# Output bias times gates joins the residual rows ahead of the expert loop; a block's activations are turned inside the next up product; loads and lists moved

## The chip, the cores and the metric

The kernel runs on one core of a Trainium2 chip. The metric is the device time in microseconds (us) of one execution. The core's engines are TensorE (PE in the profile; PEld is its loading of weights into the array), VectorE (DVE), ScalarE (ACT), GpSimd (POOL) and SyncE (SP). SyncE computes nothing here: it issues most of the transfers (DMA), in program order, and waits ahead of some of them.

## The reference, cut to what matters

One layer: attention of two kinds, and then a mixture of experts on the attended rows. The part that the change touches is the second half.

```
h = h + mix @ w_out                          # 512 token rows of 1024, the residual rows
xf = rmsnorm(h, ffn_norm)
top_val, top_idx = top_k(xf @ w_router + b_router, 4)     # 4 of 32 experts
gates = softmax(top_val)
# for each token and each of its 4 experts e:
#   act = clamped_swiglu(xf @ w1[e] + b1[e])
#   y   = act @ w2[e] + b2[e]
#   h  += gate * y
out = rmsnorm(h, final_norm)                 # in float32
```

The sum over a token's experts of gate times b2[e] depends on the gates alone. It is a product of the 512 x 32 table of gates (zero where an expert isn't chosen) with the 32 x 1024 table b2.

## The kernel before, in words

Everything is written out by hand, engine by engine, with semaphores. SBUF holds one arena that is used again and again.

**Ahead of the loop.** TensorE makes the attended rows in eight parts (`out_part`, line 1540). VectorE adds them to the residual rows `res` (line 1040). For each of four tiles of 128 tokens ScalarE and VectorE work out the root, ScalarE scales the row, GpSimd multiplies by the gain (line 559), and SyncE stores the tile in a table `xfd` in HBM (line 467). The residual rows themselves go to another table in HBM, `acc` (line 464), to which the expert loop adds. `choose(t)` finds the four experts of each token of tile t (lines 1052 to 1067) and `weigh(t)` its gates, in three bfloat16 parts (lines 1069 to 1080), both on VectorE. Then experts are ordered, tokens are counted, and tables are made that say which expert each block of 32 tokens belongs to and where the experts' weights come in the sequence of loads (lines 1111 to 1199, with small products on TensorE, lines 1612 to 1630).

**The expert loop.** Each expert's tokens are cut into blocks of 32 slots; with this input there are 81 blocks. A block's rows are gathered from `xfd` by an indirect DMA that GpSimd issues (line 567). Per block g the loop on TensorE does this (`finish_block`, line 1690, then `up_of`, line 1668):

- turn the activations of block g, two 128x128 transposes (line 1694); ScalarE copies them out as `actT` (line 811),
- turn the gathered rows of block g + 2 (`turn_x`, line 1638); ScalarE copies them (line 793),
- `slot_product` (line 1619): the token list of a block further ahead,
- four products that put b2 of block g's expert into the output bank (line 1700), from `ball`, which holds b1 and b2 in bfloat16 parts,
- `down` (line 1684): the product with w2 on top of them,
- `up` of block g + 2 (line 1657) with w1, and its bias (line 1664).

So up(g + 1) and its bias stand right ahead of finish_block(g). The products with w1 and w2 put four matmuls of 32 output columns side by side in the array (128*32 in the rows); the transposes and the token list use it in full (128*128). VectorE clamps and gates the up product (`hidden`), makes token lists (`slot_rows`, `slot_list`) and scales the result by the gates (`outputs`, line 1224); GpSimd issues the indirect DMA that adds it to `acc` (line 575).

**Weights.** One expert's weights are 12.6 MB: four loads of 2.1 MB for w1 and two for w2. SBUF holds two experts (`par` 0 and 1). SyncE loads the experts in the order of their places. Line 490 (w1) waits until the last block of the expert two places back has read that quarter of the buffer (`w1_read`), line 495 (w2) until it has read that half. The first two experts are loaded ahead of the loop: six loads early, then lines 473, 479, 480 and 482 (six more). The six early ones are w1 of the first expert and half of w1 of the second. The residual rows `res` lie where the second quarter of the second expert's w1 goes (line 479), so that load waits until they are stored.

## Time and profile before

| | us |
|---|---|
| median of 3 runs | 1412.35 |
| lowest, highest | 1410.44, 1421.33 |
| the profiled execution | 1412.71 |
| its span, first to last instruction | 1410.9 |
| TensorE busy | 1304.0 (92%) |
| TensorE loading weights into the array | 636.4 (45%) |
| VectorE busy | 662.0 (47%) |
| chain that ended last: TensorE, DMA | 83%, 10% |
| moved by DMA | 459.18 MB |

A matmul's busy time is modelled and neighbours overlap, so 92% does not say that TensorE is at its peak. The expert loop runs from about 371 us to about 1386 us of the span. In the profile's 40 slices the sixteen DMA engines are busy to a tenth or less between 106 and 212 us, and to nine tenths or more in nearly all slices of the loop. A float32 matmul leaves two records in the trace, so `x64` on line 1657 is one block's up product of 32 matmuls; a transpose leaves one.

### The profile page before, as it was taken

Reading aid. Unit: us, or ns where it says so; the run is one execution under the profiler, and the core shown is the slowest. Engines: PE = TensorE matmul, PEld = TensorE weight load, DVE = VectorE, ACT = ScalarE, POOL = GpSimd, SP = SyncE. Lnnn points to the kernel's source line nnn. Section 1 sums busy time; section 2 is a strip of 40 time slices with the busy share of each in tenths; the row PEclk is TensorE's granted clock in tenths of the full one; section 3 lists DMA queues with packets and bytes.
Section 4 is the critical chain, followed back from the end, with each engine's and each line's share of the span. In section 5 each row is a group of like instructions: output and inputs, shape, how many; then the busy total and the mean of one; then the engine's idle time right before and its main releaser. Section 6 shows DMA issues by size and latency. Waiting matters only on the chain.

```text
span 1410.9 us, 36714 instructions
## 1 busy us (share of the span) xinstructions
PE 1304.0 (92%) x13322; PEld 636.4 (45%) x13323; DVE 662.0 (47%) x2250; ACT 292.9 (21%) x579; POOL 294.5 (21%) x464
## 2 busy tenths in 40 slices
PE   7999999989489996999999999997999899999992
PEld 4756665555134442444444444442444344444441
DVE  2114334655635552555555555552555355555555
ACT  2012223424111111111111111110111111111113
POOL 5310000002112221222222222221222122222221
PEclk9999999999699998999999999998999899999996
DMA  9520003426878999999999997999999999999994
GB/s 320 149 49 1 1 0 136 167 98 260 329 314 347 416 416 421 416 417 417 418 417 416 417 415 314 378 410 420 419 418 418 418 416 416 417 416 417 400 416 167
DMA packets 59952, 459.18 MB, mean 325 GB/s; under 512 B 8692, under 2 KB 9076, under 8 KB 27156
## 3 DMA queue, kind: packets, MB, share of 16 engines
q1 hardware_dynamic: 51364, 436.12, 74.8%
q0 software_dynamic: 8176, 22.36, 6.0%
q8 instruction: 19, 0.31, 0.1%
q10 hardware_dynamic: 384, 0.32, 0.1%
q14 instruction: 9, 0.07, 0.0%
HBM read 440.26 MB, written 18.51 MB: 325 GB/s over the span
## 4 chain that ended last, share of the span: by engine, by line
PE 83%; DMA 10%; DVE 3%; issue 2%; ACT 1%; POOL 0%; ACTq 0%; SPq 0%; POOLq 0%; DVEq 0%
PE PS L1657 38%; PE PS L1684 19%; DMA sb_arena<-in_w 7%; PE PS L1322 4%; PE PS L1316 4%; PE PS L1694 2%; PE PS L1319 2%; PE PS L1320 2%; PE PS L1516 2%; PE PS L1638 1%; PE PS L1664 1%; PE PS L1700 1%; PE PS L1367 1%; PE PS L1489 1%; DMA xfd<-sb_arena 1%
## 5 line engine op out<-in xcount | busy, mean ns | idle before, releaser
L1657 PE MATMUL PS<-sb_arena,sb_work 128*32 128x512 f32 x5184 | 590.4, 606 | 35.3 <-DMA sb_arena<-in_w 28.4
L1657 PEld LDWEIGHTS PS<-sb_arena,sb_work 128*32 128x32 f32 x5184 | 188.7, 112 | 386.5 <-issue 322.1
L1684 PE MATMUL PS<-sb_arena,sb_work 128*32 128x256 f32 x5184 | 296.8, 381 | 4.5
L1211 DVE TENSOR_SCALAR sb_work<-PS 128x256 f32<-128x256 f32 x81 | 34.3, 423 | 393.9 <-PE PS L1664 393.9
L1684 PEld LDWEIGHTS PS<-sb_arena,sb_work 128*32 128x32 f32 x5184 | 166.8, 110 | 110.8 <-issue 19.4
L811 ACT ACTIVATE sb_work<-PS 128x256 f32<-128x256 f32 x81 | 31.0, 383 | 814.3 <-PE PS L1694 814.3
L1224 DVE TENSOR_SCALAR sb_work<-PS,sb_gates 32x256 f32<-32x256 f32 x324 | 155.2, 479 | 14.7 <-PE PS L1684 1.2
L566 POOL TENSOR_TENSOR sb_sm<-sb_sm 128x1 f32<-128x1 f32 x85 | 16.7, 197 | 546.5 <-DVE sb_gidx L1166 546.5
L1136 DVE TENSOR_SCALAR sb_slots<-sb_ca,sb_b,sb_rk 128x128 bf16<-128x128 f32 x340 | 95.3, 367 | 59.1 <-issue 59.1
L575 POOL DMA_INDIRECT accd<-sb_work,sb_sidc x81 | 111.3, 1374 | 12.5 <-issue 1.1
L809 ACT ACT_TABLE_LOAD x81 | 103.9, 1283 | 1.4
L567 POOL DMA_INDIRECT sb_work<-xfd,sb_gidx x85 | 85.8, 1009 | 14.1 <-issue 3.8
L1316 PE MATMUL PS<-sb_arena 128*128 128x512 f32 x128 | 58.7, 600 | 1.7 <-DVE sb_arena L874 1.7
L574 POOL TENSOR_TENSOR sb_sm<-sb_sm 128x1 f32<-128x1 f32 x81 | 15.6, 193 | 213.1 <-DVE sb_sidc L1226 213.1
L1322 PE MATMUL PS<-sb_arena 128*128 128x512 f32 x128 | 58.6, 598 | 1.0 <-DVE sb_arena L896 1.0
L927 DVE TENSOR_TENSOR_SCAN sb_arena<-sb_arena 128x1344 f32<-128x1344 f32 x8 | 23.7, 2957 | 70.1 <-ACT sb_arena L665 70.1
L1694 PEld LDWEIGHTS PS<-sb_ca,sb_work 128*128 128x128 f32 x162 | 25.5, 207 | 53.4 <-issue 53.4
L1214 DVE TENSOR_TENSOR sb_work<-sb_work,PS 128x256 f32<-128x256 f32 x81 | 34.1, 421 | 29.3 <-ACT PS L798 29.2
L1694 PE MATMUL PS<-sb_ca,sb_work 128*128 128x128 f32 x162 | 40.9, 334 | 1.2 <-issue 1.1
L1319 PE MATMUL PS<-sb_arena 128*128 128x264 f32 x128 | 39.3, 389 | 0.0
L1320 PE MATMUL PS<-sb_arena 128*128 128x264 f32 x128 | 39.0, 386 | 0.0
L1638 PE MATMUL PS<-sb_ca,sb_work 128*128 128x128 f32 x166 | 34.0, 287 | 4.8 <-DMA sb_work<-xfd,sb_gidx 4.8
(253 smaller groups left out, 1170.5 us busy)
## 6 DMA issues: line engine op xcount, KB each, us to landing
sb_arena<-in_w SPq DMA_DIRECT2D x192, 2048.0 KB
sb_arena<-in_w_in SPq DMA_DIRECT2D x6, 2048.0 KB, 21.0
sb_arena<-in_x SPq DMA_DIRECT2D x8, 512.0 KB, 7.8
sb_arena<-in_w_out SPq DMA_DIRECT2D x2, 2048.0 KB, 12.1
accd<-sb_arena SPq DMA_DIRECT2D x4, 512.0 KB, 8.9
xfd<-sb_arena SPq DMA_DIRECT2D x4, 512.0 KB, 5.2
sb_arena<-accd SPq DMA_DIRECT2D x4, 512.0 KB, 5.4
out<-sb_arena SPq DMA_DIRECT2D x4, 512.0 KB, 3.5
```

Of the source, the lines that this page charges most:

```text
L567: pool.indirect_dma_start(out=xg[b], out_offset=None, in_=xfd, in_offset=bass.IndirectOffsetOnAxis(ap=gidx[:, b:b + 1], axis=0)).then_inc( ...
L575: pool.indirect_dma_start(out=acc, out_offset=bass.IndirectOffsetOnAxis(ap=sidc[0:SLOTS, b:b + 1], axis=0), in_=yb[b], in_offset=None, com ...
L809: act.preload_act_table(ACT.Sigmoid)
L1136: nc.vector.tensor_scalar(slots[:, t, :].rearrange("p (q s) -> p q s", s=SLOTS), ca[:, C_SLOT:C_SLOT + SLOTS].unsqueeze(1).to_broadcast([P ...
L1224: nc.vector.tensor_scalar(yb[b][:, c * QD:(c + 1) * QD], PS[rows, 4, 0:QD], gates[rows, bass.ds(n, 1)], None, ALU.mult).then_inc(y_ready, 1)
L1316: last = mm(PS[:, b, :], w[:, k, f * P:(f + 1) * P], nT[:, k, META:NKEY], **io)
L1319: mm(PS[:, b, 0:n], w[:, k, f * P:(f + 1) * P], nT[:, k, 0:n], **io)
L1320: last = mm(PS[:, b + 1, 0:n], w[:, k, f * P:(f + 1) * P], nT[:, k, n:NKEY], **io)
L1322: last = mm(PS[:, b, :], nT[:, k, META + f * P:META + (f + 1) * P], w[:, k, :], **io)
L1657: last = mm(PS[group(c), b, :].rearrange("p (a n) -> p a n", a=2), xT[:, k % 2, group(k // 2)], w[:, k, :, c, :], start=k == 0, stop=False)
L1684: last = mm(PS[group(n), 4, 0:QD], actT[:, k % 2, group(k // 2)], w[:, k, n * QD:(n + 1) * QD], start=False, stop=k == KT - 1)
L1694: last = nc.tensor.transpose(PS[:, 6, j * P:(j + 1) * P], pairs(gat[b], j), ident)
```

## The change

What it does, in the order of the program:

- **Gates as a float32 table.** `weigh` keeps the gates in `gw`. For tiles 2 and 3 the weighing moves from VectorE to GpSimd; ScalarE sums their four exponentials itself, and VectorE makes only the reciprocals.
- **Last tile of rows.** Scaling and gain of tile 3 become one instruction on VectorE, in place of one on ScalarE and one on GpSimd.
- **Bias into the residual rows.** TensorE turns the gates (`turn_gates`), multiplies each tile of `res` by the identity into two PSUM banks (`rows_part`, two matmuls) and adds gates times b2 (`bias_part`, two matmuls); ScalarE copies the sum back over `res` (`rows_out`). SyncE stores the rows in `acc` after that, no longer right after they are made. b2 is loaded in float32 ahead of that; GpSimd no longer splits it, and `ball` shrinks to b1.
- **In the loop.** The four products of line 1700 are gone. The two transposes of block g's activations stand inside up(g + 1), between its sixth and seventh k step (`turn_hidden`), no longer after it.
- **Loads.** The first half of the first expert's w2 is issued once the attended rows are made; the second half once block 1's rows are turned (before: both after the stores). Of the second expert, the second quarter of w1 comes last, after all stores of `acc`; the others wait for block 1's turn, too, and not block 0's.
- **Lists.** Block 3's token list is made after block 1's up product, no longer ahead of it.

The order on TensorE inside the loop, for an even expert. Before (`1694` turns the activations, `1638` the gathered rows, `1619` is the token list, `1700` the bias, `1684` the down product, `1657` the up product):

```order
L1694 MATMUL PS<-sb_ca,sb_work 128x128 [waits act_ready]
L1638 MATMUL PS<-sb_ca,sb_work 128x128 [waits xT_ready]
L1619 MATMUL PS<-sb_g6c,sb_slots 128x6 [waits slots_ready]
L1700 MATMUL PS<-sb_ball,sb_selb 32x256 [waits sel_ready]
L1682 ISA [waits actT_ready]
L1684 MATMUL PS<-sb_arena,sb_work 32x256 [waits w2_full00]
L1684 MATMUL PS<-sb_arena,sb_work 32x256 x15
L1657 MATMUL PS<-sb_arena,sb_work 32x512 [waits w1_full00]
L1657 MATMUL PS<-sb_arena,sb_work 32x512 x7
L1657 MATMUL PS<-sb_arena,sb_work 32x512 [waits w1_full03]
L1657 MATMUL PS<-sb_arena,sb_work 32x512 x7
```

And now (`1743` turns the activations, `1728` the gathered rows, `1706` is the list, `1782` down, `1753` up):

```order
L1728 MATMUL PS<-sb_ca,sb_work 128x128 [waits xT_ready]
L1706 MATMUL PS<-sb_g6c,sb_slots 128x6 [waits slots_ready]
L1780 ISA [waits actT_ready]
L1782 MATMUL PS<-sb_arena,sb_work 32x256 [waits w2_full00]
L1782 MATMUL PS<-sb_arena,sb_work 32x256 x15
L1753 MATMUL PS<-sb_arena,sb_work 32x512 [waits w1_full00]
L1753 MATMUL PS<-sb_arena,sb_work 32x512 x7
L1753 MATMUL PS<-sb_arena,sb_work 32x512 [waits w1_full02]
L1753 MATMUL PS<-sb_arena,sb_work 32x512 x7
L1743 MATMUL PS<-sb_ca,sb_work 128x128 [waits act_ready]
L1753 MATMUL PS<-sb_arena,sb_work 32x512 [waits w1_full03]
L1753 MATMUL PS<-sb_arena,sb_work 32x512 x7
```

The two transposes moved from the head of the piece into the up product, which now runs as 24, 2 and 8 matmuls, and the bias is gone, so that the down product follows the list.

The order on TensorE between the second product of keys and block 0's up product. Before there is nothing large in it:

```order
L1614 MATMUL PS<-sb_work 32x32 [waits place_ready]
L1619 MATMUL PS<-sb_g6c,sb_slots 128x6 [waits slots_ready]
L1624 MATMUL PS<-sb_work 32x2 [waits nb_ready]
L1626 MATMUL PS<-sb_work 128x102 [waits cmp_ready]
L1638 MATMUL PS<-sb_ca,sb_work 128x128 [waits xg_in0]
L1619 MATMUL PS<-sb_g6c,sb_slots 128x6 [waits slots_ready]
L1657 MATMUL PS<-sb_arena,sb_work 32x512 [waits w1_full00,xT_ready]
```

And now, with `1667` for the residual rows and `1674` for gates times b2:

```order
L1701 MATMUL PS<-sb_work 32x32 [waits key_ready]
L1706 MATMUL PS<-sb_g6c,sb_slots 128x6 [waits slots_ready]
L1711 MATMUL PS<-sb_work 32x2 [waits cmp_ready]
L1667 MATMUL PS<-sb_arena,sb_ca 128x512 x2
L1674 MATMUL PS<-sb_arena 128x512 [waits rout_in,gt_ready]
L1716 MATMUL PS<-sb_work 128x102 [waits cmp_ready,gt_ready]
L1667 MATMUL PS<-sb_arena,sb_ca 128x512 [waits bb_out]
L1674 MATMUL PS<-sb_arena 128x512 [waits rout_in,gt_ready]
L1728 MATMUL PS<-sb_ca,sb_work 128x128 [waits xg_in0]
L1706 MATMUL PS<-sb_g6c,sb_slots 128x6 [waits slots_ready]
L1753 MATMUL PS<-sb_arena,sb_work 32x512 [waits w1_full00,bb_out,xT_ready]
```

Two of the four tiles stand here; the first stands ahead of the keys, the last between the turn of block 1's rows and its up product.

The order on SyncE from the last early loads on. Before:

```order
L464 DMA accd<-sb_arena 128x1024 [waits h_ready]
L467 DMA xfd<-sb_arena 128x1024 [waits xf_ready]
L470 DMA accd<-sb_arena 32x1024
L471 DMA xfd<-sb_arena 128x256
L473 DMA sb_arena<-in_w 128x2x2048 x2
L437 DMA sb_arena<-in_w 128x4096 [waits xf_out3,xf_out2,tab_ready,xf_out1,xT_done,xf_out0,h_out]
```

And now:

```order
L474 DMA sb_arena<-in_w 128x2x2048 [waits op_done]
L476 DMA xfd<-sb_arena 128x1024 [waits xf_last]
L479 DMA xfd<-sb_arena 128x256
L483 DMA accd<-sb_arena 128x1024 [waits bb_out]
L486 DMA accd<-sb_arena 32x1024
L483 DMA accd<-sb_arena 128x1024 [waits bb_out] x2
L493 DMA sb_arena<-in_w 128x2x2048 [waits xf_out3,tab_ready,xf_out2,xT_done,xf_out1,xf_out0]
L483 DMA accd<-sb_arena 128x1024 [waits bb_out]
L442 DMA sb_arena<-in_w 128x4096
L498 DMA sb_arena<-in_w 128x2x2048 [waits bb_done]
```

Half of w2 moved ahead of the last tile of `xfd`; the stores to `acc` (483) moved behind it, and one of them between the late loads.

```diff
+        gw = left[:, 336:464].rearrange("p (t e) -> p t e", t=TT)
+        b2f = vreg[0:NE, 3 * D:4 * D]
+        gT = vreg[0:NE, 4 * D:4 * D + T]
...
@@ -460,26 +465,39 @@
             w1_load(1, 2)
 
             for t in range(TT):
-                sp.wait_ge(h_ready, 2 * (t + 1))
-                sp.dma_start(acc[t * P:(t + 1) * P, :],
-                             res[:, t, :]).then_inc(h_out, 16)
-                sp.wait_ge(xf_ready, t + 1)
+                if t < TT - 1:
+                    sp.wait_ge(xf_ready, t + 1)
+                else:
+                    sp.wait_ge(lg_done, TT - 1)
+                    sp.dma_start(b2f, I["b2"]).then_inc(rout_in, 16)
+                    sp.wait_ge(op_done, 2 * TT)
+                    sp.dma_start(w2d(0, 0), w2v(0, 0)).then_inc(w2_full[0][0], 16)
+                    sp.wait_ge(xf_last, 1)
                 sp.dma_start(token_tile(xfd, t),
                              stage[t % 2]).then_inc(xf_out[t], 16)
 
+            sp.dma_start(xfd[Q * T:Q * T + P, :], stage[1][:, 0:QD]).then_inc(xf_out[TT - 1], 16)
+
+            def acc_out(t):
+                sp.wait_ge(bb_out, t + 1)
+                sp.dma_start(acc[t * P:(t + 1) * P, :], res[:, t, :]).then_inc(h_out, 16)
+
+            acc_out(0)
             sp.dma_start(acc[T:T + SLOTS, :], res[0:SLOTS, 0, :]).then_inc(h_out, 16)
-            sp.dma_start(xfd[Q * T:Q * T + P, :], stage[1][:, 0:QD]).then_inc(xf_out[TT - 1], 16)
-            for c in range(2):
-                sp.dma_start(w2d(0, c), w2v(0, c)).then_inc(w2_full[0][c], 16)
-            sp.wait_ge(h_out, 16 * (TT + 1))
+            acc_out(1)
+            acc_out(2)
             for t in range(TT):
                 sp.wait_ge(xf_out[t], 32 if t == TT - 1 else 16)
             sp.wait_ge(tab_ready, 1)
-            sp.wait_ge(xT_done, 1)
-            w1_load(1, 1)
+            sp.wait_ge(xT_done, 2)
+            sp.dma_start(w2d(0, 1), w2v(0, 1)).then_inc(w2_full[0][1], 16)
+            acc_out(3)
             w1_load(1, 3)
+            sp.wait_ge(bb_done, TT)
             for c in range(2):
                 sp.dma_start(w2d(1, c), w2v(1, c)).then_inc(w2_full[1][c], 16)
+            sp.wait_ge(h_out, 16 * (TT + 1))
+            w1_load(1, 1)
...
-            for t in range(TT):
+            for t in range(TT - 1):
                 pool.wait_ge(scaled, t + 1)
                 nc.gpsimd.tensor_tensor(stage[t % 2], stage[t % 2], gain, ALU.mult).then_inc(xf_ready, 1)
+
+            for t in range(2, TT):
+                row, part = e32[:, t, :], [g6[:, t, :, i] for i in range(3)]
+                pool.wait_ge(e4_ready, t + 1)
+                pool.wait_ge(msk_ready, t + 1)
+                step(nc.gpsimd.tensor_tensor(row, row, gr[:, t, :], ALU.mult))
+                pool.wait_ge(rt_ready, t - 1)
+                nc.gpsimd.tensor_scalar(gw[:, t, :], row, rt[:, t:t + 1], None, ALU.mult).then_inc(gwl_ready, 1)
+                pool.wait_ge(gwl_ready, t - 1)
...
                 act.wait_ge(e4_in, t + 1)
+                if t >= 2:
+                    step(act.activation(e4, v8[:, t, 0:TOPK], ACT.Exp, bias=ntop[:, t:t + 1],
+                                        accum_out=tot[:, t:t + 1]))
                 act.activation(e32[:, t, :], lg[:, t, :], ACT.Exp, bias=ntop[:, t:t + 1]).then_inc(e4_ready, 1)
...
-            token_scale(3)
+
+            def gates_copy(n, t0, t1):
+                act.wait_ge(gt_done, n)
+                act.activation(gT[:, t0 * P:t1 * P], PS[0:NE, 4, t0 * P:t1 * P], ACT.Copy)\
+                   .then_inc(gt_ready, 1)
+
+            def rows_out(t):
+                act.wait_ge(bb_done, t + 1)
+                b = (0, 2, 0, 3)[t]
+                act.activation(res[:, t, :].rearrange("p (b n) -> p b n", b=2), PS[:, b:b + 2, :], ACT.Copy)\
+                    .then_inc(bb_out, 1)
+
             xT_copy(1, 1)
+            act.wait_ge(xf_last, 1)
+            rows_out(3)
+            act.wait_ge(bb_out, TT)
             with act.Fori(0, (MAXBLK + 1) // 2) as i:
...
+            dve.wait_ge(e4_ready, TT - 1)
+            nc.vector.reciprocal(rt[:, 2:3], tot[:, 2:3]).then_inc(rt_ready, 1)
             token_root(3)
             choose(3)
-            weigh(2)
+            nc.vector.scalar_tensor_tensor(stage[1], res[:, 3, :], rinv[:, 3:4], gain, ALU.mult, ALU.mult)\
+                .then_inc(xf_last, 1)
+            dve.wait_ge(e4_ready, TT)
+            nc.vector.reciprocal(rt[:, 3:4], tot[:, 3:4]).then_inc(rt_ready, 1)
 
...
-            weigh(3)
-            dve.wait_ge(codes_done, 1)
+            dve.wait_ge(key_done, 1)
...
+            def turn_gates(t, dst):
+                if t < 2:
+                    pe.wait_ge(gw_ready, t + 1)
+                else:
+                    pe.wait_ge(gwl_ready, t - 1)
+                return nc.tensor.transpose(dst, gw[:, t, :], ident)
+
+            def rows_part(t):
+                b = (0, 2, 0, 3)[t]
+                if t >= 2:
+                    pe.wait_ge(bb_out, t - 1)
+                for n in range(2):
+                    mm(PS[:, b + n, :], ident, res[:, t, n * 512:(n + 1) * 512], start=True, stop=False)
+
+            def bias_part(t):
+                b = (0, 2, 0, 3)[t]
+                pe.wait_ge(gt_ready, 2 if t == TT - 1 else 1)
+                pe.wait_ge(rout_in, 64)
+                for n in range(2):
+                    last = mm(PS[:, b + n, :], gT[:, t * P:(t + 1) * P], b2f[:, n * 512:(n + 1) * 512],
+                              start=False, stop=True)
+                last.then_inc(bb_done, 1)
+
+            for t in range(TT - 1):
+                last = turn_gates(t, PS[0:NE, 4, t * P:(t + 1) * P])
+            last.then_inc(gt_done, 1)
...
+                    pe.wait_ge(h_ready, 2 * TT)
+                    rows_part(0)
                     pe.wait_ge(msk_ready, TT)
...
-            mm(PS[0:NE, 7, 0:NE], onesf, keyd, start=True, stop=True).then_inc(places_done, 1)
+            bias_part(0)
+            pe.wait_ge(key_ready, 1)
+            mm(PS[0:NE, 7, 0:NE], onesf, keyd, start=True, stop=True).then_inc(key_done, 1)
+            turn_gates(3, PS[0:NE, 4, 3 * P:4 * P]).then_inc(gt_done, 1)
+            pe.wait_ge(key_ready, 2)
+            mm(PS[0:NE, 7, 0:NE], onesf, keyd, start=True, stop=True).then_inc(key_done, 1)
 
             def slot_product(n):
                 pe.wait_ge(slots_ready, n * 5 + 5)
@@ -1620,9 +1707,12 @@
                 last.then_inc(list_done, 1)
 
             slot_product(0)
-            pe.wait_ge(nb_ready, 1)
-            mm(PS[0:NE, 7, 0:2], later, nb2, start=True, stop=True).then_inc(bs_done, 1)
             pe.wait_ge(cmp_ready, 1)
+            mm(PS[0:NE, 7, 0:2], later, nb2, start=True, stop=True).then_inc(tab_done, 1)
+            rows_part(1)
+            bias_part(1)
...
+            def turn_hidden(g, b):
+                pe.wait_ge(act_ready, g + 1)
+                for j in range(2):
+                    last = nc.tensor.transpose(PS[:, 6, j * P:(j + 1) * P], pairs(gat[b], j), ident)
+                last.then_inc(actT_done, 1)
 
             def up(g, at_place, par, b):
...
                         last.then_inc(w1_read, 1)
+                    if k == 5 and not (isinstance(g, int) and g == 0):
+                        turn_hidden(g - 1, 1 - b)
                 pe.wait_ge(sel_ready, g + 1)
...
                         last = mm(PS[group(n), 4, 0:QD], actT[:, k % 2, group(k // 2)],
-                                  w[:, k, n * QD:(n + 1) * QD], start=False, stop=k == KT - 1)
+                                  w[:, k, n * QD:(n + 1) * QD], start=k == 0, stop=k == KT - 1)
                     if k == 3:
                         last.then_inc(w2_read, 1)
                 last.then_inc(y_done, 1)
 
             def finish_block(g, at_place, par, b, i):
 
-                pe.wait_ge(act_ready, g + 1)
-                for j in range(2):
-                    last = nc.tensor.transpose(PS[:, 6, j * P:(j + 1) * P], pairs(gat[b], j), ident)
-                last.then_inc(actT_done, 1)
                 turn_x(g + 2, b, i + 1)
                 slot_product(g + 4)
                 pe.wait_ge(sel_ready, g + 2)
-                for n in range(Q):
-                    mm(PS[group(n), 4, 0:QD], selb[:, b, :], ball[:, 2 * D + n * QD:2 * D + (n + 1) * QD],
-                       start=True, stop=False)
                 pe.wait_ge(actT_ready, g + 1)
                 down(g, at_place, par)
 
+            rows_part(2)
+            bias_part(2)
             turn_x(0, 0, 0)
             slot_product(1)
             pe.wait_ge(xT_ready, 1)
+            pe.wait_ge(bb_out, 3)
             up(0, 0, 0, 0)
             pe.wait_ge(tab_ready, 1)
             nb = pe.value_load(btabi[0:1, NE - 1:NE], min_val=1, max_val=MAXBLK)
             slot_product(2)
             turn_x(1, 1, 0)
+            rows_part(3)
+            bias_part(3)
+            up_of(1, places_of(1)[0], 1)
             slot_product(3)
-            up_of(1, places_of(1)[0], 1)
+            pe.wait_ge(bb_out, TT)
             with pe.Fori(0, (MAXBLK + 1) // 2) as i:
                 for b in range(2):
                     g = 2 * i + b
@@ -1724,6 +1821,10 @@
                         pe.nop()
                         with pe.If(g + 2 < nb):
                             up_of(g + 2, following, b)
+                        with pe.Else():
+                            with pe.If(g + 1 < nb):
+                                turn_hidden(g + 1, 1 - b)
+                            pe.nop()
                         pe.nop()
                     pe.nop()
```

## Rows read from the trace of the kernel before

**Rows 1.** Stretches: us, PE, PEld, DVE, ACT, POOL busy (instructions), PEclk, DMA share, GB/s

```profile
351.10:375.00 23.90, 6.70 (x49) 2.84 (x49) 17.79 (x86) 2.86 (x4) 4.92 (x5) 0.50 0.69 257
425.30:429.10 3.80, 3.75 (x68) 2.43 (x70) 2.63 (x12) 2.25 (x4) 0.66 (x2) 1.00 0.00 0
429.10:557.60 128.50, 115.95 (x1357) 52.34 (x1348) 58.50 (x209) 20.21 (x36) 29.28 (x49) 0.95 1.01 415
557.60:854.40 296.80, 295.25 (x3620) 133.82 (x3620) 153.31 (x550) 56.15 (x100) 74.78 (x125) 1.00 1.01 417
854.50:862.20 7.70, 7.64 (x112) 3.96 (x108) 6.02 (x22) 2.25 (x4) 1.42 (x3) 1.00 0.06 18
897.60:1112.00 214.40, 197.17 (x2332) 85.74 (x2328) 98.18 (x353) 35.93 (x64) 49.47 (x82) 0.96 1.01 414
1112.00:1378.00 266.00, 264.69 (x3236) 118.92 (x3232) 137.39 (x494) 51.65 (x92) 65.80 (x110) 0.99 1.01 414
```

**Rows 2.** Timeline of SyncE: start us, us, weight loads issued (count at the end)

```profile
371.70 1.21 SPq L482 DMA_DIRECT2D sb_arena<-in_w  x2
...
428.21 2.44 SPq L495 DMA_DIRECT2D sb_arena<-in_w  x2
...
861.38 5.48 SPq L490 DMA_DIRECT2D sb_arena<-in_w  x4
...
896.80 5.47 SPq L490 DMA_DIRECT2D sb_arena<-in_w  x4
```

**Rows 3.** Timeline of TensorE at the last weight waits: start us, us, instructions, idle before

```profile
557.66 1.93 PE L1657 MATMUL PS<-sb_arena,sb_work 128*32 128x512 f32 x16 [1.42 <-DMA sb_arena<-in_w]
...
1111.58 3.64 PE L1657 MATMUL PS<-sb_arena,sb_work 128*32 128x512 f32 x16 [1.53 <-DMA sb_arena<-in_w]
...
1382.77 3.66 PE L1684 MATMUL PS<-sb_arena,sb_work 128*32 128x256 f32 x64
```

**Rows 4.** Timeline of TensorE over one block of the expert loop, to the next one

```profile
571.33 0.40 PE L1664 MATMUL PS<-sb_ball,sb_selb 128*32 128x512 bf16 x4
571.66 0.51 PE L1694 MATMUL PS<-sb_ca,sb_work 128*128 128x128 f32 x2
572.00 0.41 PE L1638 MATMUL PS<-sb_ca,sb_work 128*128 128x128 f32 x2
572.25 0.24 PE L1619 MATMUL PS<-sb_g6c,sb_slots 128*128 128x6 bf16 x4
572.42 0.29 PE L1700 MATMUL PS<-sb_ball,sb_selb 128*32 128x256 bf16 x4
572.77 3.66 PE L1684 MATMUL PS<-sb_arena,sb_work 128*32 128x256 f32 x64
...
583.11 0.40 PE L1664 MATMUL PS<-sb_ball,sb_selb 128*32 128x512 bf16 x4
```

**Rows 5.** Timeline of ScalarE in the same block: the copy of the turned activations

```profile
572.21 0.38 ACT L811 ACTIVATE sb_work<-PS 128x256 f32<-128x256 f32 x1 [9.52 <-PE PS L1694]
```

**Rows 6.** Chain of waits ahead of the loop: start us, us, what

```profile
310.16 7.15 PE PS L1540 x16
...
324.34 12.02 DMA xfd<-sb_arena
...
364.17 5.82 DMA sb_work<-xfd,sb_gidx
```

**Rows 7.** Timeline of VectorE ahead of the loop: the last mask, and around weigh(3)

```profile
352.88 1.79 DVE L1067 CAST sb_work<-sb_arena 128x32 bf16<-128x32 f32 x1
...
357.87 0.19 DVE L1073 SCALAR_TENSOR_TENSOR sb_arena<-sb_arena 128x32 f32<-128x32 f32 x1
...
359.62 0.24 DVE L1126 SCALAR_TENSOR_TENSOR sb_work<-PS,sb_work 32x32 f32<-32x32 f32 x1
```

**Rows 8.** Timeline of TensorE: block 0's up product, then block 1's gathered rows turned

```profile
371.22 8.94 PE L1657 MATMUL PS<-sb_arena,sb_work 128*32 128x512 f32 x64 [0.39 <-ACT sb_work L793]
...
380.42 0.50 PE L1638 MATMUL PS<-sb_ca,sb_work 128*128 128x128 f32 x2
```

59 lines of the change are left out of this document (35 added, 24 removed).

## The prediction

> **What bounds the kernel now.** I read the windows first. Through most of the expert loop the DMA share is 1.01 at 415 to 417 GB/s, and TensorE is busy for 295.25 of 296.80 us in the same stretch [rows 1]: transfers and TensorE are nearly in balance, so the question for each stretch is which of them waits. The stream of weights stops for 3.8 us ahead of 429.1, for 7.7 us ahead of 862.2 (both shares near 0 there, [rows 1]), and for a moment ahead of 896.8. Each time SyncE's next issue (428.21, 861.38, 896.80 [rows 2]) comes when TensorE has read a buffer, so there TensorE (or the start of the loop) sets the pace. TensorE in turn waits for weights; the last time at 1111.58, for 1.53 us [rows 3]. Behind that it runs on without a wait: the last load lands near 1378.0 [rows 1], while its reader starts at 1382.77 and needs the second half about 2 us later [rows 3].
>
> So the end is tied together like this. From 429.1 to 557.66 transfers are the bound: 24 loads in 128.5 us, 5.35 us each, from the moment at which the first of them may start. From 557.66 to the issues of 861.38 and 896.80 TensorE is the bound (about 28 blocks), then transfers again (40 loads to 1111.58), then TensorE for its last 22 blocks. A faster TensorE counts in about 50 of 81 blocks; an earlier start of the stream counts in full.
>
> **The period of a block.** From one product of line 1664 to the next it is 583.11 − 571.33 = 11.78 us [rows 4]. Up and down are most of it; the starts in between show 0.33 us for 1664, 0.34 for the two transposes, 0.25 for the turned rows, 0.17 for the list and 0.35 for the four products of line 1700 [rows 4].
>
> *Removed.* Line 1700: 0.35 us. The copy of `actT` ends at 572.21 + 0.38 = 572.59 [rows 5], 0.18 ahead of the down product at 572.77, so it lies under the bias products now. In the changed kernel the transposes are a whole half of an up product earlier and the copy is long done. The transposes go from this place: their share of it is 0.24 to 0.34 us (a pair of the same kind, line 1638, takes 0.25 to the next start), and I take 0.24. Removed from the piece between up and down: 0.59 us (0.35 and 0.24).
>
> *Added.* The same two transposes, now between k steps of up. The rows show no such place; the nearest are those where the products of 128*32 and of 128*128 follow each other. The four bfloat16 products of 1664 are 512 columns each, which a quarter of line 1657's 16 steps makes at least 0.21 us; they take 0.33 to the next start, so a turn from 128*32 to 128*128 costs about 0.12. The transposes themselves cost 0.22, and the way back 0.12 again, plus 0 to 0.23 if the first weights of the next k step can't be loaded beside a running product. That is 0.24 us (the work alone, all changes hidden) to 0.70; I take 0.51, near the middle, since one way costs what the rows show and the other isn't seen apart.
>
> Saved per block: 0.59 − 0.51 = 0.08 us. With the low end for the removal (0.44) and the high end for the addition it is −0.26, with the others +0.35.
>
> Here a rule speaks against the change. At 1664 to 1694 the trace shows the 0.12 us above [rows 4]. The Trainium skill, "TensorEngine Tiling (Array Packing)", on its tiling modes, says that a change of the mode, unlike a change of the tile within it, drains TensorE; so each block would get two more drains inside its largest product, where nothing else needed them. By that the way back would cost its high end and the saving per block would be gone or negative. That is rival B.
>
> *What hides the transposes' input.* Block g's activations must be ready at the sixth k step of up(g + 1), about 5 us into it. VectorE is busy for 153 of 297 us [rows 1], and before it had the whole of up(g + 1), 6.9 us. If `hidden` came later than that, TensorE would stand inside up. I take no wait: ScalarE waits 9.52 us for the transposes [rows 5].
>
> **Ahead of the loop.** The order of the last steps before block 0: residual rows, `xf`, its store (12.02 us [rows 6]), the gather (5.82 us at 364.17 [rows 6]), up(0).
> - The stores of `acc` no longer run beside those of `xfd`: the last tile lands about a microsecond earlier. The mask's cast at 352.88 takes 1.79 us for 128x32, where the next pass over as many elements takes 0.19 [rows 7]; I take the difference as the price of GpSimd's pass over tile 3 beside it, which is gone: 1.6 less. `weigh(3)` runs from 357.87 to 359.62, 1.75 us [rows 7], and `weigh(2)` is as long: both leave VectorE. Against that, VectorE scales tile 3: about 1.2. If all of it counts, the gather goes out 5 us earlier, at 359.
> - TensorE now has eight matmuls of 512 float32 columns for tiles 1 and 2 ahead of block 0's turn. In line 1540 eight such matmuls take 7.15 us [rows 6], 0.89 each. The first part of it runs beside the gather. At the lower granted clock they would take twice that. I put up(0) at 368.4 (371.22 before).
> - up(0) takes 8.94 us [rows 8], where in the full clock it should be 6.87 (11.78 less 1.44 for the pieces and 3.47 for down). The added products stand ahead of it, so TensorE doesn't come from idleness: 2.07 less.
>
> Together the turn of block 1's rows goes from 380.42 [rows 8] to about 376; 373 if the gather comes fully earlier, 383 if TensorE stays at the lower clock of 1.2 GHz through the new products.
>
> **The late loads.** Before, `w1_load(1, 1)` and three more went out from 371.70 [rows 2], after block 0's turn. Now five loads, with a 0.5 MB store between them, wait for block 1's turn, 376. Behind them stand the four w1 loads of the third expert, then its w2, the load that started at 429.1. Transfers: 9 × 5.35 = 48.2, store and latency 1.9 more, so it can start at about 427. TensorE's release of that half came 47.8 us after the turn of block 1's rows (428.21 − 380.42); from 376 this is 423.8, and up to 3.6 more for tile 3's four products, 427.4. Both say 427.1: the stream runs 2.0 us earlier. Ends: 5 us later (turn at 381 to 383), 5 earlier (turn at 373, tile 3 beside waits). The store of `acc` itself and the order of the last load (second quarter of w1) cost nothing where the expert's first block starts after it; that block's up is after 395 in both.
>
> **The sum.** 2.0 for the start, 0.59 for the piece that follows 557.66 directly, 50 × 0.08 = 4.0 for the blocks: 6.6 us. The profiled execution took 1412.71 us (1410.9 of span and 1.8 around it); less 6.6 is 1406.1. The median, 1412.35, lies 0.36 below the profiled one, less than I can tell: **1406**.
>
> **The rivals.**
> - *B, the change of tiling costs more.* Saving −0.2 per block: +10.0 − 2.0 − 0.6 = +7.4, **1420**. Place: inside each up product, both ways. It decides from −0.05 per block, where the sum changes its sign. Worse than 1% would need −0.33, beyond the bound. For it: two such changes in each block, in the full product. Against it: the present changes cost 0.12.
> - *C, the start is late.* From 351.1 to 375.0 the granted clock is 0.50, the level of 1.2 GHz [rows 1], and if it stays there, the new products cost double: up to 14 us for tiles 1 and 2, turn at 381 to 383. Five late loads queue behind that turn instead of four behind block 0's. Stream 5 us later: 1412.7 + 5 − 4.6 = 1413, or 1418 with no saving per block. Against it: the gather gives 4 to 5 us of cover.
> - *D, transposes nearly free.* +0.25 per block: 12.5 + 0.6 + 2.0 = 15.1, **1397.6**. Caps: between 557 and 897 no more than the stops of the stream, 7.7 and about 1.4; at the end no more than the slack of the last loads, about 5.6 us.
> - *E, nothing in the loop moves:* the saved bias and the added changes cancel, and only the start counts: **1410.5**.
>
> **How the numbers follow.** Chances: forecast 0.50, D 0.15, E 0.12, B 0.13, C 0.10. The forecast's own range is 1401 to 1411. The range for 8 in 10 reaches from 1396 (D with a little more) to 1418 (C and the milder half of B). Against no change I count 1% (14 us) as what can be told: faster than 1398.2 is D's better part and a little of the forecast, 0.15; slower than 1426.5 is the tail of B and C, 0.05; within 0.80.
>
> **What would show it right or wrong.** Period of an unstalled block 11.70 (11.98 for B, 11.53 for D). The piece from the end of one up to the start of down about 0.8 us, 1.4 before. The hidden transposes: a gap of 0.5 us inside up and no `idle before` by VectorE. The turn of block 1's rows at 376, granted clock 1.0 in up(0). First w2 load of the third expert at 427. The stop of the stream ahead of 862 shrinks from 7.7 by 28 × 0.08 = 2.2. If a wait for weights comes back after 1111, or TensorE idles inside up for `act_ready`, the prediction is wrong in its structure and not in a size.

## The result

| | us |
|---|---|
| kernel before, median of 4 runs | 1411.47 |
| changed kernel, median of 4 runs | 1425.19 |
| ratio | 1.0079 (1.0056 to 1.0102) |
| the profiled execution's span, before and changed | 1410.9 and 1422.9 |

The changed kernel is 12 to 14 us slower, and it was again on another chip: 1427.19 against 1414.75, ratio 1.0093 (1.0070 to 1.0115). The forecast was 1406, in a range up to 1418.

The profile after, in windows (the same columns as [rows 1]):

```profile
354.30:375.20 20.90, 19.06 (x53) 7.22 (x49) 11.64 (x58) 3.27 (x7) 3.93 (x8) 0.70 0.36 137
437.00:569.40 132.40, 119.35 (x1364) 47.23 (x1357) 59.52 (x214) 22.92 (x40) 29.10 (x49) 0.96 1.01 416
569.40:864.70 295.30, 291.95 (x3470) 120.28 (x3465) 150.69 (x547) 58.06 (x98) 74.47 (x125) 1.00 1.01 413
864.80:873.40 8.60, 8.60 (x122) 3.91 (x118) 5.87 (x21) 1.97 (x3) 1.42 (x3) 1.00 0.05 16
909.20:1121.00 211.80, 196.64 (x2264) 78.33 (x2256) 97.40 (x352) 37.92 (x64) 49.10 (x82) 0.97 1.01 415
1121.00:1390.30 269.30, 265.10 (x3148) 109.67 (x3148) 136.06 (x492) 54.23 (x92) 65.54 (x110) 1.00 1.01 413
```

The regime is the one of before: the stream of weights runs full from its start (437.0 now, 429.1 before), stops for 8.6 us ahead of 873.4 and for a moment ahead of 909.2, and TensorE has the last stretch. What changed are the two things that move its ends. The start is 7.8 us later. And in the stretch that TensorE bounds, 3,470 matmul records take 295.30 us. A block leaves 140 of them now and left 144 before, so that is 24.8 blocks of 11.91 us, against 25.1 blocks of 11.81 before (3,620 in 296.80 us, [rows 1]).

The timeline of TensorE over two blocks (start us, us, engine, line, ..., idle time before):

```profile
572.09 5.33 PE L1753 MATMUL PS<-sb_arena,sb_work 128*32 128x512 f32 x48
577.36 0.51 PE L1743 MATMUL PS<-sb_ca,sb_work 128*128 128x128 f32 x2
577.79 1.92 PE L1753 MATMUL PS<-sb_arena,sb_work 128*32 128x512 f32 x16
579.53 0.40 PE L1762 MATMUL PS<-sb_ball,sb_selb 128*32 128x512 bf16 x4
579.86 0.51 PE L1728 MATMUL PS<-sb_ca,sb_work 128*128 128x128 f32 x2
580.21 0.24 PE L1706 MATMUL PS<-sb_g6c,sb_slots 128*128 128x6 bf16 x4
580.38 3.66 PE L1782 MATMUL PS<-sb_arena,sb_work 128*32 128x256 f32 x64
583.86 5.33 PE L1753 MATMUL PS<-sb_arena,sb_work 128*32 128x512 f32 x48
...
591.29 0.40 PE L1762 MATMUL PS<-sb_ball,sb_selb 128*32 128x512 bf16 x4
591.98 0.50 PE L1728 MATMUL PS<-sb_ca,sb_work 128*128 128x128 f32 x2 [0.28 <-issue]
592.31 0.24 PE L1706 MATMUL PS<-sb_g6c,sb_slots 128*128 128x6 bf16 x4
592.49 3.66 PE L1782 MATMUL PS<-sb_arena,sb_work 128*32 128x256 f32 x64
595.96 4.47 PE L1753 MATMUL PS<-sb_arena,sb_work 128*32 128x512 f32 x40
```

From one up product to the next it is 583.86 − 572.09 = 11.77 us and then 595.96 − 583.86 = 12.10. Up now takes 579.53 − 572.09 = 7.44 us with the transposes inside it. From its bias to the down product it is 0.85 us (579.53 to 580.38), where it was 1.44 [rows 4]. In the second block the same piece has 0.28 us of idle time ahead of line 1728, "issue": TensorE waits for no semaphore that the profile shows. Experiment 6 shows that its own sequencer, which works through the loop's branches and register operations, is late. This stands at the place where the loop jumps back, and so in every second block. Of the blocks between 560 and 850 us the even ones have a median of 11.76 and the odd ones of 12.10, and the second trace of this kernel has 11.76 and 12.06.

TensorE ahead of the loop: 1667 and 1674 are the residual rows and gates times b2, 1728 the turned rows of block 0, 1753 its up product, and the last two rows are block 4's list and block 0's down product (the turn of block 1's rows stood at 385.69):

```profile
362.40 2.92 PE L1667 MATMUL PS<-sb_arena,sb_ca 128*128 128x512 f32 x4
365.25 3.78 PE L1674 MATMUL PS<-sb_arena 32*128 32x512 f32 x4
...
369.35 3.78 PE L1667 MATMUL PS<-sb_arena,sb_ca 128*128 128x512 f32 x4
373.07 2.20 PE L1674 MATMUL PS<-sb_arena 32*128 32x512 f32 x4
375.20 0.51 PE L1728 MATMUL PS<-sb_ca,sb_work 128*128 128x128 f32 x2
...
376.66 8.77 PE L1753 MATMUL PS<-sb_arena,sb_work 128*32 128x512 f32 x64 [0.87 <-ACT sb_work L841]
...
403.43 0.25 PE L1706 MATMUL PS<-sb_g6c,sb_slots 128*128 128x6 bf16 x4 [2.86 <-DVE sb_g6c L1196]
403.66 5.35 PE L1782 MATMUL PS<-sb_arena,sb_work 128*32 128x256 f32 x64
```

SyncE: the first late load, the third expert's w2 and the issue that ends the long stop, which answer to [rows 2]:

```profile
386.26 0.38 SPq L493 DMA_DIRECT2D sb_arena<-in_w  x1
...
435.95 2.11 SPq L513 DMA_DIRECT2D sb_arena<-in_w  x2
...
872.48 6.02 SPq L508 DMA_DIRECT2D sb_arena<-in_w  x4
```

Against the first trace of the kernel before, this is where the 12.0 us of span come from, by the start of a transfer or of an up product:

| place | before | changed | difference |
|---|---|---|---|
| block 0's up | 371.2 | 376.7 | +5.5 |
| block 2's up | 398.7 | 408.8 | +10.1 |
| third expert's w2 begins to move | 429.2 | 437.0 | +7.8 |
| stream moves again after its long stop | 862.4 | 873.5 | +11.1 |
| block 59's up, behind the last wait for weights | 1120.2 | 1129.6 | +9.4 |
| block 80's up | 1367.6 | 1380.1 | +12.5 |
| end of the span | 1410.9 | 1422.9 | +12.0 |

So 7.8 us come from the start and 3.3 + 0.3 from the first stretch of TensorE (the 0.3 at the short stop, which ended at 897.8 before and at 909.2 now). Then 2.0 are given back while transfers bound, 3.1 come from the last 21 blocks (21 × 0.15 = 3.2), and behind block 80 0.5 are given back. A second trace of each shows how firm that is: the start was 432.3 and 437.0, so it costs 5 to 8 us, block 80 stood at 1368.5 and 1379.4.

### The profile page after: what moved, and what is told of

The parts are those of the page before. It is cut to its first block, busy times and chain, and to the rows that moved or that the text cites. A ratio compares the mean times of both kernels' runs of the same rounds, so it can differ in the third digit from the quotient of the medians.

```text
span 1422.9 us, 36230 instructions
## 1 busy us (share of the span) xinstructions
PE 1332.5 (94%) x13034; PEld 609.1 (43%) x13035; DVE 654.8 (46%) x2237; ACT 307.0 (22%) x588; POOL 285.8 (20%) x468
## 4 chain that ended last, share of the span: by engine, by line
PE 86%; DMA 8%; DVE 3%; issue 2%; ACT 1%; POOL 0%; DVEq 0%; SPq 0%; ACTq 0%; POOLq 0%
PE PS L1753 38%; PE PS L1782 19%; DMA sb_arena<-in_w 7%; PE PS L1373 4%; PE PS L1379 4%; PE PS L1728 2%; PE PS L1743 2%; PE PS L1376 2%; PE PS L1377 2%; PE PS L1597 2%; PE PS L1573 2%; PE PS L1762 1%; PE PS L1424 1%; PE PS L1546 1%; PE PS L1476 1%
## 5 line engine op out<-in xcount | busy, mean ns | idle before, releaser
L1753 PE MATMUL PS<-sb_arena,sb_work 128*32 128x512 f32 x5184 | 601.9, 605 | 30.2 <-DMA sb_arena<-in_w 25.9
L1753 PEld LDWEIGHTS PS<-sb_arena,sb_work 128*32 128x32 f32 x5184 | 161.2, 111 | 357.9 <-issue 303.9
L1782 PEld LDWEIGHTS PS<-sb_arena,sb_work 128*32 128x32 f32 x5184 | 161.1, 110 | 101.2 <-issue 3.0
L1281 DVE TENSOR_SCALAR sb_work<-PS,sb_gates 32x256 f32<-32x256 f32 x324 | 155.1, 479 | 11.1 <-PE PS L1782 2.0
L846 ACT ACTIVATE PS<-sb_work 128x256 f32<-128x256 f32 x81 | 31.4, 388 | 190.7 <-DVE sb_work L1268 190.7
L978 DVE TENSOR_TENSOR_SCAN sb_arena<-sb_arena 128x1344 f32<-128x1344 f32 x8 | 23.7, 2958 | 70.2 <-ACT sb_arena L695 70.2
L1743 PEld LDWEIGHTS PS<-sb_ca,sb_work 128*128 128x128 f32 x162 | 25.3, 206 | 69.3 <-issue 69.3
L1728 PEld LDWEIGHTS PS<-sb_ca,sb_work 128*128 128x128 f32 x166 | 26.2, 207 | 65.9 <-issue 65.9
L1728 PE MATMUL PS<-sb_ca,sb_work 128*128 128x128 f32 x166 | 41.7, 333 | 11.5 <-issue 10.0
L1743 PE MATMUL PS<-sb_ca,sb_work 128*128 128x128 f32 x162 | 40.9, 335 | 0.0
L1376 PE MATMUL PS<-sb_arena 128*128 128x264 f32 x128 | 39.3, 389 | 0.0
```

The lines of the kernel that those rows point to most:

```text
L1281: nc.vector.tensor_scalar(yb[b][:, c * QD:(c + 1) * QD], PS[rows, 4, 0:QD], gates[rows, bass.ds(n, 1)], None, ALU.mult).then_inc(y_ready, 1)
L1376: mm(PS[:, b, 0:n], w[:, k, f * P:(f + 1) * P], nT[:, k, 0:n], **io)
L1728: last = nc.tensor.transpose(PS[:, 7, j * P:(j + 1) * P], pairs(xg[b], j), ident)
L1743: last = nc.tensor.transpose(PS[:, 6, j * P:(j + 1) * P], pairs(gat[b], j), ident)
L1753: last = mm(PS[group(c), b, :].rearrange("p (a n) -> p a n", a=2), xT[:, k % 2, group(k // 2)], w[:, k, :, c, :], start=k == 0, stop=False)
L1782: last = mm(PS[group(n), 4, 0:QD], actT[:, k % 2, group(k // 2)], w[:, k, n * QD:(n + 1) * QD], start=k == 0, stop=k == KT - 1)
```

## Experiments on the loop

**1. The transposes back at the head.**

```diff
-                    if k == 5 and not (isinstance(g, int) and g == 0):
-                        turn_hidden(g - 1, 1 - b)
...
+                pe.wait_ge(act_ready, g + 1)
+                for j in range(2):
+                    last = nc.tensor.transpose(PS[:, 6, j * P:(j + 1) * P], pairs(gat[b], j), ident)
+                last.then_inc(actT_done, 1)
                 turn_x(g + 2, b, i + 1)
```

> The changed kernel with the two transposes of a block's activations back at the head of the piece between up and down, and the added else branch gone; all else as changed. In the changed kernel the trace shows 11.76 us for one block and 12.10 for the next, the second with about 0.3 us of TensorE idle behind the up bias, at the loop's jump back. Theory J (the jump back is no longer covered, since the first instruction behind it now has register work and a wait for the gather in front of it): no idle time, both blocks about 11.61 (11.78 less the 0.17 us by which the down product could start after the copy of the turned activations, 572.59 against 572.77). About 50 of the 81 blocks count: 1425.2 - 50 x 0.31 = 1410, or 1413 if the stops of the weight stream (8.8 and 1.2 us) cap it. Theory T (the change of tiling inside up is what costs): the same period here, but it would come from both blocks alike. Rival: the idle time stays at the jump even with the transposes at the head, 12.0 for every second block, 1421.

Measured: 1423.46, ratio to before 1.0051 (1.0027 to 1.0075); both blocks 11.89 us, no idle time at the jump, but 0.38 us of it in each block ahead of the down product. The period fell by 0.04 a block (from the mean of 11.76 and 12.10), not by 0.31: my price for the piece was wrong. It is slower than the kernel before, which has four products more.

**2. The four bias products alone taken out** of the kernel before.

```diff
-                for n in range(Q):
-                    mm(PS[group(n), 4, 0:QD], selb[:, b, :], ball[:, 2 * D + n * QD:2 * D + (n + 1) * QD],
-                       start=True, stop=False)
```

The down product's first k step now opens the sum, and b2 is missing from the result.

> The kernel before without the four products of line 1700, so that b2 is left out of the result and nothing else changes. What are they worth? If the down product waits for the copy of the turned activations in their place: 11.61 us a block, 0.17 saved. If the copy is no bound: 11.43. Time 1411.5 less 50 x 0.17 = 8.5: 1403; with 0.35 a block the stops of the stream (7.7 and 1.4 us) and 5.6 us of slack at the end cap it at about 1397. Rival (the transfers bound everything): 1411.

Measured: 1421.71 in one run, with before at 1415.54 (median of 19) on that chip. One run doesn't settle the time, since single runs of before reached 1422.02 there. The period does: both blocks take 11.89 for 11.78. Less work makes a block slower. Its TensorE and its ScalarE in the piece (the list, then the down product; the copy of the turned activations):

```profile
612.40 0.50 PE L1694 MATMUL PS<-sb_ca,sb_work 128*128 128x128 f32 x2
612.74 0.40 PE L1638 MATMUL PS<-sb_ca,sb_work 128*128 128x128 f32 x2
612.98 0.24 PE L1619 MATMUL PS<-sb_g6c,sb_slots 128*128 128x6 bf16 x4
613.61 3.66 PE L1684 MATMUL PS<-sb_arena,sb_work 128*32 128x256 f32 x64 [0.39 <-ACT sb_work L811]
```

```profile
612.94 0.38 ACT L811 ACTIVATE sb_work<-PS 128x256 f32<-128x256 f32 x1 [9.62 <-PE PS L1694]
```

The copy ends at 612.94 + 0.38 = 613.32, and down starts at 613.61, 0.29 later, and 1.21 us behind the transposes. In the kernel before the copy ended at 572.59 and down started at 572.77, 1.11 us behind them [rows 4, 5]. So the way from the transposes through ScalarE to the down product is what sets this piece; the bias products stood under it at no cost, and they even had TensorE at work when the copy was ready. From the end of the copy to down it is 0.28 to 0.33 us in every block between 560 and 850 us of this kernel and of experiment 1's, where TensorE stands idle, and 0.18 in every one of the kernel before, of experiment 4's and of those in experiment 7, where it doesn't. So starting from idle goes with 0.11 us more; why isn't shown.

**3. The transposes inside up alone**, in the kernel before (the edit of experiment 1 the other way round, with the else branch).

> The kernel before with only one part of the change: the two transposes stand inside the next up product, with the else branch for the last block. The four bias products of line 1700, the loads, the residual rows and the lists are as before. The changed kernel shows 0.57 us more in up and 0.59 less between up and down, of which 0.35 were the bias products. Here the bias stays: +0.57 - 0.24 - 0.13 (its wait for the copy) = +0.20 to +0.33 a block, and 0.3 more in every second block if the idle time at the jump is there too. Theory J with the dear transposes: 12.0 to 12.1 and 12.3 to 12.4, 1411.5 + 50 x 0.4 = 1431 (1428 to 1436). If the slow-down of the changed kernel sat in what comes ahead of the loop alone: 1412.

Measured: 1428.93, 1.0101 (1.0059 to 1.0142); 11.85 and 12.15 us.

```profile
601.06 0.40 PE L1672 MATMUL PS<-sb_ball,sb_selb 128*32 128x512 bf16 x4
601.39 0.51 PE L1638 MATMUL PS<-sb_ca,sb_work 128*128 128x128 f32 x2
601.73 0.24 PE L1619 MATMUL PS<-sb_g6c,sb_slots 128*128 128x6 bf16 x4
601.90 0.29 PE L1704 MATMUL PS<-sb_ball,sb_selb 128*32 128x256 bf16 x4
602.02 3.63 PE L1692 MATMUL PS<-sb_arena,sb_work 128*32 128x256 f32 x64
```

With the copy long done, the four bias products cost 0.12 us (601.90 to 602.02), against 0.35 where the down product behind them waited for it. From the up bias to down it is 0.96 us. So the move takes 0.48 out of the piece and puts 0.57 into up; the bias then takes out 0.11 more.

**4. An else branch that does nothing**, in the kernel before.

```diff
                         with pe.If(g + 2 < nb):
                             up_of(g + 2, following, b)
+                        with pe.Else():
+                            with pe.If(g + 1 < nb):
+                                pe.nop()
+                            pe.nop()
```

> The kernel before with an else branch that does nothing behind `if g + 2 < nb`, holding an inner if, as in the changed kernel. Theory E (the else branch adds jumps to every block, and these make the idle time of 0.3 us in every second block): 11.78 and 12.1 us, 1411.5 + 50 x 0.16 = 1419.5. Theory J (the jump was there before and is only uncovered by what stands behind it): both blocks 11.78, 1411.5, no idle time behind the up bias.

Measured: 1416.54, 1.0011 (0.9994 to 1.0029); both blocks 11.78. The group of the transposes, the first matmuls behind the jump (busy, mean ns, idle before), of this kernel, and line 1728's group of the changed one:

```profile
L1694 PE MATMUL PS<-sb_ca,sb_work 128*128 128x128 f32 x162 | 40.9, 334 | 1.7 <-issue 1.7
```

```profile
L1728 PE MATMUL PS<-sb_ca,sb_work 128*128 128x128 f32 x166 | 41.7, 333 | 11.5 <-issue 10.0
```

1.7 us of idle time in the whole run against 10.0 of "issue". The branch alone makes no idle time where the transposes stand at the head. That it has no part in it where they stand inside up isn't shown by this: there the branch always stands too (see experiment 6).

**5. The token list ahead of the turned rows**, in the changed kernel.

> The changed kernel with the token list ahead of the turned gathered rows in the loop's piece. In the changed kernel 0.15 to 0.5 us of idle time stand at the jump back of the loop, ahead of the turned rows, whose first instruction has a register operation and a wait on the gather ahead of it; with the two transposes of the activations at the head there was none, and an added else branch alone made none. Theory W (it is this register work and wait that come too late): the list has none of it, and the period of every second block falls from 12.1 to 11.8. Theory G (what covers the jump is work for TensorE: the queue runs dry in the jump whatever stands first, and only the sequence of matmuls ahead of it, the short up bias, matters): still 12.0 to 12.1.

Measured: 1419.46 in one run; 11.78 and 12.15 us. The idle time now stands ahead of the list, so theory W falls as I put it. It isn't a clean test, as the list's first matmul has a register instruction in front of it too. The transposes at the head have one as well (line 1692), with no idle time, and that speaks against W once more.

**6. Two idle transposes at the head**, in the changed kernel.

```diff
+                for j in range(2):
+                    nc.tensor.transpose(PS[:, b, j * P:(j + 1) * P], pairs(gat[b], j), ident)
                 turn_x(g + 2, b, i + 1)
```

> The changed kernel with two more transposes at the head of the loop's piece, which turn the same activations into a PSUM bank that nobody reads; the real ones stay inside the up product. They cost TensorE 0.24 to 0.34 us where it doesn't wait. Theory J (the jump back takes longer than the queue ahead of it lasts, and the transposes at the head, which need no register work of their own, used to cover it): no idle time ahead of the turned rows, both blocks 12.0 to 12.1. Theory I (the turn inside up itself makes the idle time, since it sets TensorE's sequencer back, whatever stands at the head): 12.0 to 12.1 and 12.3 to 12.4, with idle time of 0.2 to 0.3 behind the up bias in every second block.

Measured: 1429.81 in one run; 12.01 and 12.09 us.

```profile
L1791 PE MATMUL PS<-sb_ca,sb_work 128*128 128x128 f32 x162 | 40.9, 334 | 3.6 <-issue 3.1
L1728 PE MATMUL PS<-sb_ca,sb_work 128*128 128x128 f32 x166 | 33.8, 285 | 0.0
```

The difference between the two blocks falls from 0.34 to 0.08. Work at the head covers most of the jump (theory J). There are still 3.1 us of "issue" ahead of it in the run, against 1.1 in the kernel before.

The traces hold TensorE's branches and register operations too, which the views leave out, and they show the rest. Behind the issue of up, the sequencer goes through a chain of these: out of the branch of this block, at every second block back to the loop's start, and to the next wait. This chain starts 2.39 us ahead of the up bias in the kernel before and in experiments 1 and 4, and 1.71 us ahead of it in the changed kernel and in experiments 3, 5 and 6, the same to 0.01 us in each of the 22 to 24 blocks from 575 to 850 us. So the turn inside up takes 0.68 us from the sequencer's lead, with and without transposes at the head (theory I). At a jump the chain takes 2.32 us in the kernel before (median), and 2.59 with the idle else branch of experiment 4, where the lead still covers it. In the changed kernel the last operation ahead of line 1728 starts some 0.6 us behind the start of the bias at a jump, and at 591.88 in the block shown; the bias is done at 591.69, and the matmul starts at 591.98. The idle time is thus a shorter lead, a chain that the else branch makes 0.27 us longer, and no transposes at the head to cover it. How much each would make alone isn't tested, and why the turn shortens the lead is open.

**7. The cover kept, the waste taken out.** If the way through ScalarE sets the piece, then what TensorE must do anyway belongs under it. Two kernels move the up bias (b1) there: in the changed kernel, transposes back at the head, it opens the sum of block g + 2; in the kernel before it closes the sum of block g + 1. The first one also makes the selector a step earlier on VectorE. Of the second one's edit, the part where the up bias now stands:

```diff
                 slot_product(g + 4)
+                with pe.If(g + 1 < nb):
+                    up_bias(g + 1, 1 - b)
+                pe.nop()
                 pe.wait_ge(sel_ready, g + 2)
```

> The changed kernel with the two transposes back at the head, and the four products of the up bias (b1) of block g + 2 opening its sum between block g's token list and its down product, no longer closing it behind the up product. The selector is made a step earlier on VectorE. Without anything in that place the down product stood 1.21 us behind the transposes, 0.38 of it idle for the copy. Theory C (the piece between up and down is set by the copy of the turned activations; what stands under it costs nothing, and up's own tail loses 0.21 to 0.33): up to transposes 0.12 instead of 0.33 + 0.12, transposes to down 1.11 to 1.21: period 11.55 to 11.7, 50 x (11.92 - 11.62) = 15 less than the changed kernel: about 1410, which is 0 to 5 less than before. Rival (each product costs its own time wherever it stands): 11.89 + 0 = 11.9, 1423 as with the transposes alone back.

> The kernel before with one edit: the up bias (b1) of block g + 1 closes its sum behind block g's token list, ahead of the products of line 1700, behind a branch that leaves it out where there is no such block. Everything else, the prologue too, as before. Theory C: period 11.55 to 11.65 us instead of 11.78, and no idle time at the jump, since the transposes head the piece: 50 x 0.18 = 9 less than before. Rival 1 (each product costs its time wherever it stands): 11.78, no change. Rival 2 (the branch in the piece stalls TensorE's sequencer, as at the jump): 11.9 to 12.1, 6 to 16 more than before.

Measured: 1406.14, 0.9946 (0.9927 to 0.9964), and 1404.88, 0.9931 (0.9910 to 0.9953), with before at 1414.75. Both have 11.56 us in even and odd blocks. The second one, which still has the four b2 products (1708) and now the b1 products (1655) too:

```profile
611.60 7.05 PE L1666 MATMUL PS<-sb_arena,sb_work 128*32 128x512 f32 x64
618.59 0.51 PE L1699 MATMUL PS<-sb_ca,sb_work 128*128 128x128 f32 x2
618.93 0.40 PE L1638 MATMUL PS<-sb_ca,sb_work 128*128 128x128 f32 x2
619.17 0.24 PE L1619 MATMUL PS<-sb_g6c,sb_slots 128*128 128x6 bf16 x4
619.35 0.40 PE L1655 MATMUL PS<-sb_ball,sb_selb 128*32 128x512 bf16 x4
619.58 0.28 PE L1708 MATMUL PS<-sb_ball,sb_selb 128*32 128x256 bf16 x4
619.70 3.66 PE L1689 MATMUL PS<-sb_arena,sb_work 128*32 128x256 f32 x64
623.17 1.05 PE L1666 MATMUL PS<-sb_arena,sb_work 128*32 128x512 f32 x8
```

From up to the transposes there is nothing left, and from these to down it is 1.11 us, as before. With and without the b2 products the period is the same to 0.01 us: in this place they are free. The long stop of the stream shrank from 7.7 us in the kernel before to about 3, so TensorE's 0.22 us a block arrived, and most of what there was to gain in that stretch is used up.

## Experiments on the start

**8. Each kernel once more, for its trace.**

> The changed kernel once more, beside the kernel before on the same chip, for its trace: what of its lateness ahead of the loop comes again? In the first two traces the first gather is issued at 364.2 (before) and 364.4 (changed), and the first load of the third expert's w2 starts at 429.2 and 437.0. In two other kernels with the prologue of before the gather came at 366 to 371 and the load at 434 to 435. Theory S (the start of the changed kernel is late by its own work): load 71 to 73 us behind the first gather, against 63 to 68 where the prologue is that of before. Theory R (all of it is scatter of the granted clock from one execution to the next): the same distance in both. Periods again 11.76 and about 12.1 us; about 12 us above the kernel before.

> The kernel before once more, for a second trace of it. Theory S: load 63 to 66 us behind the first gather, both blocks 11.78 us. Theory R: 70 or more.

Measured: changed 1427.19; before 1413.17 in this run. From the first gather's issue to the load it is 437.0 − 364.2 = 72.8 and 432.3 − 365.9 = 66.4 us; in the first traces 72.6 and 65.0. By this distance theory S holds. Over all kernels it is 68.7 to 74.1 us in experiments 1, 5, 6 and 10 (loads early; list back), which have the changed kernel's steps, and 62.9 to 68.5 in the four with those of before.

But the two traces of the changed kernel are not all that its steps can do. The kernel of experiment 5 differs from it only inside the loop, and the one with the list back only behind block 1's turn. Their gathers went out at 359.0 and 359.7, up(0) started at 368.6 and 369.2, and the stream at 429.1 and 428.4, no later than in the kernel before. Where they differ from the changed kernel's traces is the granted clock: from 365 to 375 us it is 0.83 in both, and 0.57 and 0.59 in the changed kernel's two. All eight runs of the changed kernel took 1424.7 to 1430.2 us and these two took 1419.46 and 1421.41 in one run each, so whether its start is late by its own timing or by chance isn't settled.

**9. Without the new products ahead of the loop.** Four columns stand in for each tile, so b2 is missing from the result.

> The changed kernel without the rows and bias products ahead of the loop (a product of four columns and a copy of four columns stand in for each tile, so b2 is left out of the result); the waits, the order of the loads and the lists are as changed. In two traces of the changed kernel block 0's up starts at 376.4 and 376.7, the third expert's w2 at 437.0 in both. The stream's start is there the half of block 2's down product. Theory P (the 12 us of these products between 354 and 375 hold up block 0, whose gathered rows were there at about 370): up(0) at 371, turn of block 1's rows at 380, w2 load at 431 to 432, time 1426 - 5.5 = 1420. Theory L (the late loads and the moved list hold the start, the products are hidden by waits): up(0) still 375 or more or the load still at 436 to 437, 1426.

Measured: up(0) at 366.1, 5.0 us behind the gather's issue where it is 12.2 in the changed kernel, and the load at 431.3, 5.7 us earlier. That is theory P's figure, but the gather was issued 3.3 us earlier in this trace too (361.1). From gather to load it is 70.2 us against 72.6, so the products are worth 2.4 to 5.7 us of the start. The time is 1425.07 in one run, no better. Half of the earlier start was given back in the loop (block 59's up at 1126.6, block 80's at 1377.4, where the changed kernel had 1129.6 and 1380.1) and the rest behind it: from block 80's up to the end it is 45.8 us here, and 42.8 and 45.7 in the two traces of the changed kernel.

**10. Loads early; list back; both.**

> The changed kernel with the late loads as early as in the kernel before: the second half of the first expert's w2 and the last quarter of the second expert's w1 wait for block 0's turned rows alone (not block 1's), and the store of the last tile of residual rows stands behind the second expert's w2. Theory L (the late loads are what starts the stream late): the load of the third expert's w2 moves from 437 to about 431, time 1420. Theory Q (TensorE's own way to the half of block 2's down product sets the start, and it waits for no weights on it): the load stays at 436 to 437 and the time at 1426.

> The changed kernel with block 3's token list back ahead of block 1's up product. In the changed kernel it stands behind it, block 4's list follows at once and waits 2.86 us for VectorE's next slot rows, and the down product behind it takes 5.35 us, where it takes 3.66 later, at a lower granted clock. Theory M (this wait and the lower clock behind it lie on the way to the stream's start): block 1's up to block 2's up 18.3 becomes about 13.5, though block 1's up may start later by the wait of the list (0 to 3 us): the w2 load 2 to 5 us earlier, 432 to 435, time 1421 to 1424. Theory L: no change, 437 and 1426.

Measured: loads early, the load at 437.2, 1424.96. TensorE's half of block 2's down product sets the start there (theory Q). With the list back, the load at 428.4, 1421.41, one run each. But this kernel had a better start altogether: its gather was issued at 359.7. Its products for tile 2:

```profile
363.93 1.98 PE L1667 MATMUL PS<-sb_arena,sb_ca 128*128 128x512 f32 x4
365.84 1.98 PE L1674 MATMUL PS<-sb_arena 32*128 32x512 f32 x4
...
369.21 8.64 PE L1753 MATMUL PS<-sb_arena,sb_work 128*32 128x512 f32 x64 [0.87 <-ACT sb_work L841]
```

1.98 us for four records, where the changed kernel's trace had 3.78 and 2.20; the granted clock from 365 to 375 us is 0.83, and was 0.57 there. The nine loads go out from 378.7 and reach the third expert's w2 50 us later, so transfers set the start here. The kernel of experiment 5 has as good a start with the list at its late place, and its stream starts at 429.1, 70.0 us behind the gather against 68.7: next to full transfers the moved list is worth about 1 us. What its wait of 2.86 us is worth where TensorE sets the start isn't shown.

The kernel of experiment 7 (transposes at the head, up bias as cover) with the list back:

> The changed kernel with the transposes back at the head, the up bias of block g + 2 opening its sum ahead of the down product (as in the kernel that took 11.56 us a block), and block 3's token list back ahead of block 1's up product. Block 1's up to block 2's up was 15.6 us there, with 2.62 of waiting for VectorE, and 13.6 in a kernel with the list back. If that wait lies on the way to the stream's start: 2 less than the 1406 of the kernel without this edit, 1404, ratio to before 0.992. If the start is given back by longer stops of the stream: 1406, 0.994.

Measured: 1403.96, 0.9942 (0.9921 to 0.9962). Block 2's up came 4.3 us earlier than in experiment 7, the stream's start stayed (428.7 for 428.9). SyncE of this kernel shows why: the issue of that w2 is at 422.75, but its packets start at 428.7, behind the nine loads.

```profile
378.66 0.38 SPq L493 DMA_DIRECT2D sb_arena<-in_w  x1
...
422.75 2.40 SPq L513 DMA_DIRECT2D sb_arena<-in_w  x2
```

And with the loads early on top of it:

> The kernel with the transposes at the head, the up bias as their cover and block 3's list put back, and on top of it the late loads early: the second half of the first expert's w2 and the last quarter of the second expert's w1 wait for block 0's turned rows alone, and the last store of residual rows stands behind the second expert's w2. Without that edit the third expert's w2 was issued at 422.8 and its transfer began at 428.7, behind nine loads from 378.7 on. Theory B (TensorE's way and the transfers are in balance there, so that only both edits together move the start): the transfer begins 4 to 5 us earlier, 424, the stream keeps this up to its stop near 857, and the time falls by 3 to 5 to 1399 to 1401, ratio to before 0.990. Rival: the earlier start is given back by a longer stop, 1404, 0.994. The granted clock ahead of the loop shifts each start by up to 5 us from one execution to the next, so the distance from block 0's turned rows to the transfer counts: 60.5 there, 56 by theory B.

Measured: 1402.79, 0.9918 (0.9892 to 0.9944). From the turn of block 0's rows to the transfer it is 58.0 us (370.0 to 428.0) against 61.2 (367.5 to 428.7): 3.2 of the 4 to 5 expected, since the second quarter of w1 still waits for the last store. By their intervals the last two can't be told apart. Each against the kernel before on its own chip, this one is at 0.9918 and the changed kernel at 1.0093, 1.7% apart.

## Why the prediction was wrong

The forecast for the bound, for which stretches count and for the distances was right: 24 loads in 128 us (437.0 to 565.1), 9 loads in 50 us, a long stop near 862 that answers to TensorE. Two terms had the wrong sign, the saving per block and the gain at the start.

**The period: forecast 0.08 saved per block, measured 0.15 lost** (11.78 against the mean of 11.76 and 12.10). The difference of 0.23, times my 50 blocks, is 11.5 of the 19 us by which I missed.
- "Removed from the piece between up and down: 0.59 us" is what happened (1.44 to 0.85). But I took line 1700 as 0.35 us of work. It was 0.12 of work and a wait for the copy. "It lies under the bias products now" was in my text, and I read it as a small slack of 0.18; it was the bound of the whole piece. The split matters: either part of the change alone makes a block slower (11.89 and 11.85).
- The added transposes were put at 0.51 (0.24 to 0.70) and cost 0.57 a block. With 0.24 for their own work (an estimate), the two changes of tiling and whatever else the place costs come to 0.33, about 0.17 each and not 0.12; no run tells the parts of this apart. The Trainium skill, "TensorEngine Tiling (Array Packing)", says in its part on tiling modes that such a change drains the engine. The traces fit that, with 0.57 above the 0.51 that I took, but not the high end of 0.70 that I had put to it.
- The idle time of 0.34 in every second block was in no term. The else branch is in my diff and I gave it no row; alone it makes no idle time, but it makes the sequencer's chain 0.27 us longer. I costed a moved step by its own duration, and not by what it covered at its old place: the loop's jump back. Nor did I ask what the turn inside up does to the sequencer, whose lead shrank by 0.68 us. This is the failed step, 0.17 of the 0.23 us per block; the other 0.06 are the transposes' place.

**The start: forecast 2.0 earlier, measured 5 to 8 later.**
- The gather was to go out at 359 and went at 364.4. Both traces of the changed kernel are late before anything changed runs: one and the same VectorE instruction starts at 256.1 and 255.9, and at 252.3 and 254.1 in the two traces of the kernel before. Nine other kernels with the new steps ahead of the loop issue the gather at 359.0 to 363.8, and those with the old ones, the first traces included, at 364.2 to 371.1. The kernels of experiments 5 and 10 (list back), whose steps up to there are this kernel's, have that instruction at 252.4 and 252.7 and the gather at 359.0 and 359.7, as forecast. So the gain of some 5 us exists and this kernel's traces don't get it; whether by its own timing or by chance the runs don't settle.
- "At the lower granted clock they would take twice that" was the right sentence and the wrong choice: lines 1667 and 1674 took 12.7 us for tiles 1 and 2, not 7.2, and stood ahead of block 0. Taken out, the start is 2.4 to 5.7 us earlier.
- up(0) was to take 6.87 and took 8.77, although TensorE had been busy for 19.06 of the 20.9 us in front of it: the granted clock was 0.57 from 365 to 375 us, with TensorE busy all the time, and 0.81 across up(0). That it doesn't come from idleness did not keep the clock up.
- The moved list was not in the sum at all. It shows as 2.86 us of waiting for VectorE, then a down product of 5.35 for 3.66. What this cost isn't shown (about 1 us where transfers set the start).
- The 50 us from the first late load to the third expert's w2 were right: 386.3 to 437.0.

**The rivals.** B (−0.2 a block, 1420) and C (start 5 later, 1413 to 1418) both came true in size, or nearly. For B that is luck: its cause, dearer changes of tiling, is 0.06 of the 0.23 us, and by it alone a block would still have saved 0.02 (0.59 − 0.57); the rest is idle time that no rival had. C's cause, the new products at the lower clock, is in the traces. I gave them 0.13 and 0.10 as if they excluded each other. Their causes are different, one in the loop and one ahead of it, so they add: 1412.7 + 7.5 + 5 = 1425. A range built from one failure at a time ended at 1418 for that reason.

## What to carry to other kernels

Before taking an operation away, or moving it, find what its neighbour waits for: if a wait ends inside or right behind it, its duration in the timeline is cover and not cost, and the cheaper edit is to move other needed work under that wait. Price a move by what stood hidden under the old place (a copy, a jump of the loop) as well as by what it costs in the new one. And where the risks of a change lie in different stages, add them for the end of the range.

## What was not expected of the hardware

- Leaving out four matmuls of 256 columns made a block 0.11 us slower: a down product that starts from an idle TensorE came 0.29 us behind the end of the copy it waits for (median of the blocks), and 0.18 us where the engine was at work until then.
- A jump back of the loop cost TensorE nothing with two transposes first behind it, and about 0.3 us without them and with the activations turned inside up. That turn cost the sequencer 0.68 us of its lead over the up bias (1.71 for 2.39), in every block of every kernel that has it.
- Unchanged code came up to 3.8 us later at 256 us in one trace than in another, with a granted clock of 0.94 for 1.00 in the first 30 us and 0.83 for 0.91 between 240 and 270.
